# Attention in halves of the array and retention's new rows in column quarters, in a two-layer decoder trunk

## What is computed

```python
# attention, for each block of 128 queries over 256 keys
s = einsum('...qkgd,...skd->...kgqs', qg, k) * (ATTN_HEAD_DIM ** -0.5)     # scores
w = p / (sum(p) + exp(sink - m))
o = einsum('...kgqs,...skd->...qkgd', w, v)                                # values
# retention: the new rows read the updated state of their own sequence
s = s * chunk_decay + einsum('bjhd,bjhe->bhde', ki * k_decay, vi)
o = ... einsum('bihd,bhde->bihe', qi, s) * q_decay
o = (o - mean(o)) * rsqrt(var(o) + GN_EPS)
```

## Time and profile before

| | |
|---|---|
| median of 3 runs | 3008.26 us (3005.65 to 3009.05) |
| profiled execution, its own time | 3004.96 us |
| its span, first to last instruction | 3003.2 us |
| TensorE busy | 2891.7 us, 96%, 17936 matmuls |
| VectorE, ScalarE, GpSimd busy | 52%, 30%, 19% |
| mean granted TensorE clock | 0.986 of full |

### The profile page before, as it was taken

One profiled execution on the slowest core, in us unless ns is written; L12 is line 12 of the kernel. 1 busy time (PEld: TensorE's weight loads), 2 busy tenths in 40 slices (PEclk: granted clock), 3 DMA queues, 4 the chain that ended last, 5 costly groups with the idle time before them and its releaser, 6 DMA issues.

```text
span 3003.2 us, 44032 instructions
## 1 busy us (share of the span) xinstructions
PE 2891.7 (96%) x17936; PEld 2751.4 (92%) x17936; DVE 1558.1 (52%) x3113; ACT 903.4 (30%) x1683; POOL 585.0 (19%) x496
## 2 busy tenths in 40 slices
PE   7999989999999999999999999999999999999996
PEld 6888879999999999998988888888899999999995
DVE  5565577544444454515345353376675444444445
ACT  4344345222211122322433433422143122222213
POOL 2333352000000002403223222111141000000012
PEclk9999999999999999999999999999999999999997
DMA  3210100111111111234555555665511111111101
GB/s 127 75 29 16 44 30 29 65 49 43 43 50 50 43 53 53 71 125 142 180 178 174 176 173 176 208 202 186 167 48 57 43 57 43 43 57 43 43 25 57
DMA packets 192489, 260.47 MB, mean 87 GB/s; under 512 B 29281, under 2 KB 150753, under 8 KB 192257
## 3 DMA queue, kind: packets, MB, share of 16 engines
q1 hardware_dynamic: 127392, 196.16, 20.6%
q10 hardware_dynamic: 64896, 61.50, 5.9%
HBM read 191.50 MB, written 68.20 MB: 86 GB/s over the span
## 4 chain that ended last, share of the span: by engine, by line
PE 83%; DVE 6%; issue 5%; ACT 3%; POOL 2%; DMA 1%; SPq 0%; ACTq 0%; POOLq 0%; DVEq 0%
PE bank L482 27%; PE bank L484 26%; PE bank L483 26%; PE bank L916 2%; ACT y L1008 1%; DVE bank L1450 1%; PE bank L596 1%; PE bank L535 1%; DVE n_sq L1443 1%; DVE y L1457 1%; DVE wl L1403 1%; ACT xh L1012 0%; PE bank L882 0%; DVE y L1428 0%; DVE xl L1465 0%
## 5 line engine op out<-in xcount | busy, mean ns | idle before, releaser
L482 PE MATMUL bank<-xh,wh 128*128 128x344 f32 x3624 | 1170.9, 323 | 19.4 <-DVE y L1428 8.2
L483 PE MATMUL bank<-xl,wh 128*128 128x344 f32 x3624 | 1159.3, 320 | 0.0
L484 PE MATMUL bank<-xh,wl 128*128 128x344 f32 x3624 | 1159.3, 320 | 0.0
L482 PEld LDWEIGHTS bank<-xh,wh 128*128 128x128 f32 x3624 | 682.9, 188 | 46.6 <-issue 20.2
L483 PEld LDWEIGHTS bank<-xl,wh 128*128 128x128 f32 x3624 | 682.6, 188 | 4.9
L484 PEld LDWEIGHTS bank<-xh,wl 128*128 128x128 f32 x3624 | 682.9, 188 | 0.0
L1428 DVE TENSOR_TENSOR y<-bank,y 128x344 f32<-128x344 f32 x648 | 324.8, 513 | 228.5 <-PE bank L484 228.4
L2049 POOL TENSOR_TENSOR f_hl<-f_cv,f_hh 128x344 fp32r<-128x344 f32 x132 | 123.0, 933 | 1265.5 <-ACT f_hh L1126 1265.5
L482 PE MATMUL bank<-f_hh,wh 128*128 128x344 f32 x1056 | 339.8, 322 | 0.0
L484 PE MATMUL bank<-f_hh,wl 128*128 128x344 f32 x1056 | 337.4, 319 | 0.0
L483 PE MATMUL bank<-f_hl,wh 128*128 128x344 f32 x1056 | 337.1, 319 | 0.0
(11 more groups left out here) (214 smaller groups left out, 3680.3 us busy)
## 6 DMA issues: line engine op xcount, KB each, us to landing
raw<-in_w SPq DMA_DIRECT2D x216, 512.0 KB, 3.6
scratch_qkvg<-p_plain ACTq DMA_DIRECT2D x96, 172.0 KB, 2.2
r_s<-in_state_in SPq DMA_DIRECT2D x32, 512.0 KB, 3.6
out_state_s<-r_s ACTq DMA_DIRECT2D x32, 512.0 KB, 5.5
scratch_qkvg<-p_rot ACTq DMA_DIRECT2D x24, 344.0 KB, 3.3
r_cxq<-scratch_qkvg SPq DMA_DIRECT2D x32, 256.0 KB, 5.6
r_cxv<-scratch_qkvg SPq DMA_DIRECT2D x32, 256.0 KB, 5.8
r_cxg<-scratch_qkvg SPq DMA_DIRECT2D x32, 256.0 KB, 5.2
```

The lines of the kernel that those rows point to most:

```text
L482: pe.matmul(out, ah, bh, start=(k == 0), stop=False)
L483: pe.matmul(out, ah, bl, start=False, stop=False)
L484: mm = pe.matmul(out, al, bh, start=False, stop=(k == n - 1))
```

## The change

`scores` issues the same passes in another order: for each pass the even and the odd head of a pair in turn. `values` drops the split of v and of the probabilities: v stands once as float32 (`a_v`), the probabilities as float32 (`a_pt`), and each half of the array's columns (output partitions 0 to 63, 64 to 127) gets a float32 product over the two heads that belong there (256 columns). `pt_lo` and `a_vl` go; TensorE waits for ScalarE's `pt_in` and, in `project`, for `rope_t`. `sample_out` issues four products of 256 columns where two of 512 stood, one for each half of the value's columns and each half of the key, into partitions from 0, 32, 64 and 96; VectorE adds the two parts of each in `sample_norm`. `r_ob` now lies in the place of `r_ga`.

```diff
-                pe.wait_ge(T["v_free"], NB * g + b - 1)
+                pe.wait_ge(T["rope_t"], (NB + 1) * g + b - 1)
...
-            for h in range(GH):
-                r = slice(HD * (h % 2), HD * (h % 2) + HD)
-                q = slice(W * (h // 2), W * (h // 2) + W)
+            for j in range(2):
+                q = slice(W * j, W * j + W)
                 for k0, at, n in pieces:
-                    o = bank[3 + h % 2][:, (h // 2) * 256 + at:(h // 2) * 256 + at + n]
-                    mm = accumulate(pe, o, [(K.a_qh[r, q], K.a_ql[r, q], K.a_kh[r, k0:k0 + n], K.a_kl[r, k0:k0 + n])])
+                    passes = ((K.a_qh, K.a_kh), (K.a_qh, K.a_kl), (K.a_ql, K.a_kh))
+                    for n_pass, (qs, ks) in enumerate(passes):
+                        for odd in range(2):
+                            r = slice(HD * odd, HD * odd + HD)
+                            mm = pe.matmul(bank[3 + odd][:, j * 256 + at:j * 256 + at + n], qs[r, q], ks[r, k0:k0 + n],
+                                           start=(n_pass == 0), stop=(n_pass == 2))
...
-            pe.wait_ge(T["pt_lo"], NB * g + b + 1)
+            pe.wait_ge(T["pt_in"], NB * g + b + 1)
...
-            accumulate(pe, bank[7][:, :], terms).then_inc(T["heads"], 1)
+            first = 0 if b else 1
+            for t in range(first, 2):
+                for odd in range(2):
+                    mm = pe.matmul(bank[7][HD * odd:HD * odd + HD, 0:2 * W], K.a_v[:, (b - 1 + t) % VR, :],
+                                   K.a_pt[:, t, :].rearrange("p (j h n) -> p j h n", j=2, h=2)[:, :, odd, :],
+                                   start=(t == first), stop=(t == 1))
+            mm.then_inc(T["heads"], 1)
...
-            after(pe, R["x_ga"], h)
-        for j in range(2):
-            mm = pe.matmul(xB[0:NS, :], K.qm[:, j, b, :], K.s0[:, i % 2, j, :], start=(b == 0 and j == 0),
-                           stop=(b == NS - 1 and j == 1))
+            after(pe, R["x_sum"], h)
+        for half in range(2):
+            c = slice(half * RV // 2, (half + 1) * RV // 2)
+            for j in range(2):
+                at = 32 * (2 * half + j)
+                mm = pe.matmul(xB[at:at + NS, c], K.qm[:, j, b, :], K.s0[:, i % 2, j, c], start=(b == 0), stop=(b == NS - 1))
...
-                a = act.activation(K.a_pth[:, t, :], bank[5 + t][:, :], ACT.Copy)
+                a = act.activation(K.a_pt[:, t, :], bank[5 + t][:, :], ACT.Copy)
...
-                a = dve.tensor_tensor(K.a_ptl[:, t, :], bank[5 + t][:, :], K.a_pth[:, t, :].bitcast(F32), ALU.subtract)
...
+        after(dve, R["ob_lo"], i)
         dve.tensor_scalar(K.ga[:, :], bank[6][:, :], K.st[:, 0:1], K.st[:, 5:6], ALU.subtract, ALU.mult).then_inc(R["ga"], 1)
...
     def sample_norm(h):
+        c0, c1 = slice(0, RV // 2), slice(RV // 2, RV)
         dve.wait_ge(R["x_o"], NB * (h + 1))
-        dve.bn_stats(K.xst6[:, :], bank[7][0:NS, :]).then_inc(R["x_stats"], 1)
+        dve.wait_ge(R["xv_out"], 16 * min(h + 2, RH))
+        dve.tensor_copy(K.xu[:, c0], bank[7][32:32 + NS, c0])
+        dve.tensor_copy(K.xv[:, c1], bank[7][64:64 + NS, c1])
+        dve.tensor_copy(K.xu[:, c1], bank[7][96:96 + NS, c1]).then_inc(R["x_part"], 1)
+        dve.wait_ge(R["x_part"], h + 1)
+        dve.tensor_tensor(K.xu[:, c0], bank[7][0:NS, c0], K.xu[:, c0], ALU.add)
+        dve.tensor_tensor(K.xu[:, c1], K.xv[:, c1], K.xu[:, c1], ALU.add).then_inc(R["x_sum"], 1)
+        dve.wait_ge(R["x_sum"], h + 1)
+        dve.bn_stats(K.xst6[:, :], K.xu[:, :]).then_inc(R["x_stats"], 1)
```

More of the change, by code:

```diff
@@ L280 @@
         "p_in prod rot plain out_r0 out_r1 out_p0 out_p1").split()
-ATT_SEMS = ("table_in turn_in cache_in rope_t v_hi v_fp v_free qk back t_hi t_lo score shifted small small2 expd "
-            "inv probs pt pt_hi pt_lo heads heads_hi heads_lo kv_out win_out s_sc s_scc "
+ATT_SEMS = ("table_in turn_in cache_in rope_t v_in v_fp qk back t_hi t_lo score shifted small small2 expd "
+            "inv probs pt pt_in heads heads_hi heads_lo kv_out win_out s_sc s_scc "
             "s_tr s_mx s_ex s_p s_pt s_ptc s_o s_of s_oh s_ol dchain").split()
@@ L285 @@
             "s_hi s_lo stats small root ga back ob ob_hi ob_lo oh_out ol_out st_in0 st_in1 st_out0 st_out1 decay outer "
-            "x_in x_ing masks rows xv xv_out vb x_o x_stats x_small x_root x_ga x_back xo xo_hi xo_lo xoh_out xol_out "
+            "x_in x_ing masks rows x_part x_sum xv xv_out vb x_o x_stats x_small x_root x_ga x_back xo xo_hi xo_lo xoh_out xol_out "
             "s_out oin0 oin1 oin2 oin3 oin4 oin5").split()
@@ L369, in build @@
         sb = place(REGION)
-        K.a_vh = sb("a_vh", [P, VR, 2, HD], F32R)
-        K.a_vl = sb("a_vl", [P, VR, 2, HD], F32R)
+        K.a_v = sb("a_v", [P, VR, HD])
         K.a_vf = sb("a_vf", [P, HD])
@@ L376, in build @@
         K.a_st = sb("a_st", [P, 8, GH])
-        K.a_pth = sb("a_pth", [P, 2, GH * W], F32R)
-        K.a_ptl = sb("a_ptl", [P, 2, GH * W], F32R)
+        K.a_pt = sb("a_pt", [P, 2, GH * W])
         K.a_oh = sb("a_oh", [P, 2, TOK], F32R)
@@ L592, in turn_probs @@
             if b >= 1:
-                pe.wait_ge(T["pt_lo"], NB * g + b)
+                pe.wait_ge(T["pt_in"], NB * g + b)
             for t in range(0 if b else 1, 2):
@@ L626, in sample_turn_probs @@
             pe.wait_ge(T["s_p"], g + 1)
-            pe.wait_ge(T["pt_lo"], NB * (g + 1))
+            pe.wait_ge(T["pt_in"], NB * (g + 1))
             pe.transpose(bank[5][:, 0:32], K.a_sp[:, 0:W], ident[0:32, 0:32])
@@ L1084, in attention @@
         heads_hi(NB - 2)
-        pt_hi(NB - 1)
+        pt_in(NB - 1)
         split_next(1)
@@ L1528, in inverse @@
             dve.reciprocal(K.a_st[:, 7, :], K.a_st[:, 6, :]).then_inc(T["inv"], 1)
-        def pt_lo(b):
-            dve.wait_ge(T["pt_hi"], NB * g + b + 1)
-            for t in range(0 if b else 1, 2):
-                a = dve.tensor_tensor(K.a_ptl[:, t, :], bank[5 + t][:, :], K.a_pth[:, t, :].bitcast(F32), ALU.subtract)
-            a.then_inc(T["pt_lo"], 1)
         def heads_lo(b):
@@ L1603, in attention @@
                 heads_lo(t - 4)
-            if t >= 3:
-                pt_lo(t - 3)
         t_lo(NB)
@@ L1611, in attention @@
         shift(NB - 1)
-        pt_lo(NB - 2)
         add_y(4, 6)
@@ L1618, in attention @@
         sample_shift()
-        pt_lo(NB - 1)
         add_y(8, 10)
@@ L1883, in sample_norm_rest @@
         dve.wait_ge(R["x_small"], 2 * h + 2)
-        dve.wait_ge(R["xv_out"], 16 * min(h + 2, RH))
-        dve.tensor_scalar(K.xv[:, :], bank[7][0:NS, :], K.xst[:, 0:1], K.xst[:, 4:5], ALU.subtract, ALU.mult)\
+        dve.tensor_scalar(K.xv[:, :], K.xu[:, :], K.xst[:, 0:1], K.xst[:, 4:5], ALU.subtract, ALU.mult)\
            .then_inc(R["x_ga"], 1)
```

31 lines of the change are left out of this document (12 added, 19 removed).

## The result

The changed kernel takes 2966.98 us, the median of four runs (2965.45 to 2970.56), against 3007.15 in four runs of the kernel before beside it (3005.65 to 3009.05): ratio 0.9868, 95% interval [0.9851, 0.9885]. The forecast was 2958.6. From profile to profile the span falls from 3003.2 to 2966.1 us, 37.1, where the sum had 49.7. Faster was right, and the time lies inside the range. It also lies inside the likeliest case's own range (2951 to 2968), but by 1 us only, and a repeat of the same program gave 2971.9, so that much was luck. A quarter of the gain is missing by the profiles (37.1 of 49.7), a fifth by the medians (40.2 of 49.7).

A forecast was written before the change was run, and what follows sets the result against it. TensorE, busy 96% of the span, was taken as the bound. Attention 23.2 plus retention 26.5 gave 49.7 us off 3004.96, 2955.3; with 3.3 for the median of runs, 2958.6 us, range 2950 to 2990.

The forecast's parts named there:

- likeliest case: Column places overlap fully or nearly so: 2951 to 2968 us, chance 0.66.
- g: Retention, each `sample_out` call: TensorE's product falls from 1.72 to 0.46 us, 1.25 us won.
- x: Attention, each `values` block: last q and k transpose to scores falls from 1.58 to 1.16 us, 0.42 won.
- (a): Rival: column tiles start only in program order, so only neighbours overlap; 31.7 us off, 2976.6 us; chance 0.17 including mixtures.
- (b): Rival: column tiles do not overlap at all; 1.2 us more, 3009.5 us; chance 0.11.
- (c): Rival: no overlap, and each move between column tiles costs 0.09 us; 3022.7 us; chance 0.06.
- 0.28 a wrapped block: Attention scores whose keys wrap in the ring: pairing passes removes the second head's lag, 0.28 us twice a group.
- VectorE's relief at the waits for y: Behind the attention loop, dropped subtractions shrink two TensorE waits by 1.2 us each: 2.4 a group, 1.2 more in the last.
- The added 2.0 us in period 25: Retention: `sample_norm`'s added VectorE operations take 2.0 us four times, showing only in period 25, where VectorE is late already.
- Eleven calls of `sample_out`: Retention calls followed by `inner`, which needs `r_qkl`: five only lengthen the wait, six give 0.39 us each, 2.3 in all.
- nothing else is late: 21 x 1.25: Retention: 21 of 32 `sample_out` calls have enough TensorE work behind them to keep their full saving, 26.2 us.
- rival (d): Full overlap with one or two half-clock stretches gone (2955 to 2957 us) or added (to 2962); no separate chance.

The follow-up runs named there:

- The scores alone: Kernel before with only the scores' passes of the two row halves issued in pairs: 3005.1 us against 3005.3, ratio 0.9997.
- k ahead of v: Queries first kernel, with k split ahead of v on ScalarE and VectorE: 2943.0 us, ratio 0.9796.
- queries first: Changed kernel with the next period's queries ahead of this period's state on ScalarE and GpSimd: 2949.5 us, ratio 0.9814.

## Why the forecast was right, and where it was not

**Right.** The overlap of column places: g = 1.27 (1.25), x = 0.37 (0.42); rivals (a), (b) and (c) are out by the timeline. (The scores alone rule out strict program order for row halves; for column places it is the eight records in 0.79 us.) The scores at nothing but 0.28 a wrapped block. `a_prob` as what holds turns of the loop (t = 6). VectorE's relief at the waits for y. The added 2.0 us in period 25, and the other three norms covered. Eleven calls of `sample_out` whose saving goes into longer waits for `r_qkl`: 17.7 us in 12, where it was 6.8 in 6, and the experiment that removes these waits gives 17.5 back.

**Wrong.** First, the step "nothing else is late: 21 x 1.25". It followed one releaser of `inner`, `r_qkl`, and took no row for the other, `r_kdl`. Towards the `inner` of periods 6, 14 and 22 only 0.55 us came through of each call's 1.25 (from the `inner` of period 5 to that of 6 it is 25.66 us, before 26.21), 2.1 us in all. k ahead of v removed this wait. The six calls priced at 0.39 were right: 0.37 to 0.40 in five of them, 0.12 in the sixth.

Second, rival (d) was mis-sized: "one or two more" half-clock stretches, to 2962. There were two more in periods 0 to 22 (3.1 us) and four more in periods 23 to 25 (some 5.4 us). Third, the wait for the DMA in period 23 had no term and grew by 1.2. By stage: 1.9 are missing in the attention, 5.7 up to period 23 (2.1+3.1 and 0.5 over), 6.4 from there to period 26; 1.5 came on top behind it, where a stretch of the kernel before is absent. That is luck and not the change: three of the five traces with the old `sample_out` have two stretches there, the other two none. That is 12.5 of the 12.6 us between 49.7 and 37.1. The sum closes for this pair of traces; the stretches make another pair differ by a few us in each stage. The forecast summed waits as if the work behind them ran at the same speed.

What stays open is why the clock falls behind a given wait and not behind another: equal waits in equal code have a stretch in one group or trace and not in the next. That the changed kernel has more of them in periods 23 to 25 is shown by seven traces; that its longer waits cause them is argued from where they stand, and only the joint effect is shown (waits for `r_qkl` away: the early ones gone, 17.5 us).

Of the attention's 1.9, six times four blocks at an x smaller by 0.05 make 1.2. Two readings in the prediction are slightly off and change nothing: the two score rows that it shows stand 0.22 us apart, and only the four behind them 0.12; and the change of the array's form is 0.24-0.16 = 0.08, not 0.09.

## What to carry to other kernels

Before counting a faster product at its full price, list for each point that it brings forward all that the next instruction waits for, each with its margin, and the second in line too; here two swaps of order were worth 17.5 and some 5 to 6.5 us, together more than half of what the change gave. Where VectorE or GpSimd prepares both what TensorE needs next and what it needs later, put the next first. Price a wait with the clock behind it: in this kernel a stretch at half clock, where one comes, adds 1.6 us to a wait of 1 to 3. And don't read a gain of a few us in one stage off a single pair of traces: the same attention code differed by 3.2 us between two of them.

## What the hardware showed that was not expected

Four column places of fp32 products run beside each other without loss: 1.72 us less the 1.27 won leaves 0.45, about two records of 0.215 one after the other, and two places take 0.41 more. Halving the passes to 128 columns changes nothing. The Trainium skill ("TensorE: Matmul & The Clock Gate", Measured speedup vs the span model) has 2.38 times for three column tiles; no run here has three, and four gave 1.72/0.45 = 3.8 times.

The same small VectorE product of two tiles in SBUF, the masks' `r_qm`, takes between 0.21 and 2.41 us in one trace, by what GpSimd does beside it. With the old order the second one of period 9 ran 1.30 us beside `r_qkl`; with queries first it runs 2.41 beside `r_sl`, and TensorE waits 1.4 us for `r_state` behind it. The timeline of POOL and DVE with queries first:

```profile
1541.90 2.38 POOL L2089 TENSOR_TENSOR r_sl<-r_state,r_sh 128x1024 fp32r<-128x1024 f32 x1
1541.94 2.41 DVE L1842 TENSOR_TENSOR r_qm<-r_m,r_xs 128x64 f32<-128x64 f32 x1
```

The Trainium skill ("GPSIMD Engine Reference", Specifications) says that GpSimd's SBUF interfaces are shared with VectorE and contend with its instructions of two SBUF inputs; the rows agree. That 2.41 stands beside 2.38 suggests, but doesn't show, a wait for the whole of GpSimd's instruction.
